# The experts of three routed layers, worked off with the four groups in turn instead of one group after the other

## The reference

```python
g_prob = softmax(t @ rg_w + rg_b); g_p, g_idx = top_k(g_prob, 1)      # one of 4 groups
e_logits = (t @ re_w + re_b).reshape(n_tok, 4, n_experts // 4)[own group]
e_p, e_idx = top_k(softmax(e_logits), 2)                              # two experts of that group
...
y = (silu(x @ w_gate[e]) * (x @ w_up[e])) @ w_down[e]                 # hidden width 512
out[token] += g_p * e_p / sum(e_p) * y
```

| layer | blocks of each expert | sum |
|---|---|---|
| 0 | 3 3 2 3 / 2 2 2 2 / 3 3 3 3 / 2 3 3 3 | 42 |
| 1 | 1 1 1 2 4 5 1 4 / 2 1 2 1 1 3 2 1 / 1 1 1 1 1 1 1 1 / 2 1 1 1 2 1 1 2 | 51 |
| 2 | 2 2 1 2 1 1 2 1 / 2 1 1 2 2 2 2 1 / 1 1 3 3 1 2 5 2 / 1 1 1 1 1 1 1 1 | 51 |

## Time and profile before

### The profile page before, as it was taken

The page is one execution under the profiler, slowest core; times in us unless marked ns, Lnnn a source line. Parts: engine busy times, 40 slices in busy tenths (PEclk is TensorE's granted clock), DMA queues, the critical chain, the costliest instruction groups (busy, mean ns, idle before and its releaser), DMA issues. The chain is left out here.

```text
span 2638.0 us, 87033 instructions
## 1 busy us (share of the span) xinstructions
PE 2273.6 (86%) x37784; PEld 1652.5 (63%) x37785; DVE 1061.3 (40%) x2686; ACT 549.8 (21%) x1197; POOL 290.6 (11%) x487
## 2 busy tenths in 40 slices
PE   8997988788899888999767779978889988788986
PEld 4445546566688655777545535868876466566763
DVE  1306442222553844333212257457675353222323
ACT  2126211111400731111001031034432111111111
POOL 1001223223100010000000010012333100000001
PEclk9998999999999999999989889989999999999998
DMA  8602169999404007979999942010001289999996
GB/s 339 268 32 96 50 242 337 410 382 366 171 32 155 9 19 296 382 292 428 429 429 428 427 151 72 33 58 3 3 5 66 88 343 428 428 428 428 409 428 249
DMA packets 92275, 635.63 MB, mean 241 GB/s; under 512 B 22741, under 2 KB 43481, under 8 KB 58090
## 3 DMA queue, kind: packets, MB, share of 16 engines
q1 hardware_dynamic: 48272, 584.61, 53.8%
q0 software_dynamic: 12752, 29.14, 3.5%
q10 hardware_dynamic: 31114, 19.86, 2.4%
HBM read 588.42 MB, written 45.12 MB: 240 GB/s over the span
## 5 line engine op out<-in xcount | busy, mean ns | idle before, releaser
L1323 PE MATMUL ps<-ring,arena 128*32 128x128 f32 x13184 | 410.7, 284 | 111.3 <-DMA ring<-in_experts 73.8
L1323 PEld LDWEIGHTS ps<-ring,arena 128*32 128x32 f32 x13184 | 380.8, 115 | 154.7 <-issue 74.2
L1534 DVE TENSOR_TENSOR arena<-arena,ps 128x64 f32<-128x64 f32 x292 | 64.8, 222 | 587.5 <-ACT arena L1382 587.5
L1382 ACT ACTIVATE arena<-ps 128x64 f32<-128x64 f32 x292 | 65.5, 224 | 1075.1 <-PE ps L1323 950.0
L1334 PE MATMUL ps<-ring,arena 128*32 128x256 f32 x3296 | 204.4, 382 | 35.1 <-DVE arena L1537 20.0
L1300 PE MATMUL ps<-x_tok,arena 128*32 128x256 f32 x3456 | 212.0, 384 | 14.7 <-DVE arena L1437 8.3
L1323 PE MATMUL ps<-arena 128*32 128x128 f32 x5504 | 174.4, 286 | 48.3 <-DMA arena<-in_experts 36.3
L1323 PEld LDWEIGHTS ps<-arena 128*32 128x32 f32 x5504 | 161.4, 115 | 67.5 <-DMA arena<-in_experts 42.3
L1334 PEld LDWEIGHTS ps<-ring,arena 128*32 128x32 f32 x3296 | 107.1, 110 | 111.3 <-issue 27.8
L1273 PE MATMUL ps<-ring,arena 128*128 128x512 f32 x384 | 172.0, 604 | 3.4 <-PEq L2861 1.7
L1300 PEld LDWEIGHTS ps<-x_tok,arena 128*32 128x32 f32 x3456 | 116.3, 112 | 72.4 <-issue 21.8
(11 more groups left out here) (506 smaller groups left out, 3234.9 us busy)
## 6 DMA issues: line engine op xcount, KB each, us to landing
ring<-in_experts SPq DMA_DIRECT2D x165, 2048.0 KB, 21.7
arena<-in_experts SPq DMA_DIRECT2D x50, 2048.0 KB, 24.3
xt_mem<-in_experts SPq DMA_DIRECT2D x25, 2048.0 KB
ring<-in_mixer_chunks SPq DMA_DIRECT2D x24, 2048.0 KB, 11.8
xybuf<-arena ACTq DMA_DIRECT2D x602, 32.0 KB, 6.8
xybuf<-arena SPq DMA_DIRECT2D x1, 9216.0 KB, 51.8
xbuf<-arena SPq DMA_DIRECT2D x1, 9216.0 KB, 31.7
arena<-xbuf POOLq DMA_DIRECT2D x168, 32.0 KB, 6.5
```

Of the source, the lines that this page charges most:

```text
L1323: ins = pe.matmul(ps[at, 2 + half, 0:P], xg[:, k, :], w_gu[half][:, k, q, :], start=(k == 0), stop=(k == NK - 1))
L1382: act.activation(silu_g[:, half, :], ps[:, 2 + half, 0:HALF], ACT.Silu).then_inc(s_silu[half], 1)
L1534: dve.tensor_tensor(hidden[:, half, :], silu_g[:, half, :], ps[:, 2 + half, HALF:P], ALU.mult)\
```

## The change

Two lines of data flow change. In `expert_chunks`, the experts of an array are put into the order: first expert of each of the four groups, second expert of each group, and so on (old number g·E/4+e moves to place 4e+g). In the router, the masked logits `es` are written in the same order, so that picks, counts, table, slots and loops follow it by themselves. The input `el` and the router's weights keep their order. No instruction, transfer, semaphore or loop is added or taken away; every expert keeps its tokens, its three chunks and its number of blocks, and the output is the same sum.

```diff
-                    link(dve.tensor_tensor(es.rearrange("p j (g e) -> p j g e", g=G),
+                    link(dve.tensor_tensor(es.rearrange("p j (e g) -> p j g e", g=G),
                                            el.rearrange("p j (g e) -> p j g e", g=G),
                                            pen.unsqueeze(3).to_broadcast([P, NT, G, EPG]), ALU.add))
...
-    return np.ascontiguousarray(np.concatenate([gu, dn], axis=1))
+    chunks = np.concatenate([gu, dn], axis=1)
+
+    return np.ascontiguousarray(chunks.reshape(4, E // 4, *chunks.shape[1:]).swapaxes(0, 1).reshape(chunks.shape))
```

## The result

The changed kernel takes 2620.43 us (median of 4 runs, 2612.69 to 2623.02) against 2642.53 us: ratio 0.9912, 95% interval 0.9894 to 0.9930. That is 22 us less, where 22.1 were forecast (2619.9 us). The profiled execution took 2620.4 us, its span is 2618.7.

The account below looks back on a forecast made before the run. The loops of layers 1 and 2 were taken as mostly bound by weight loads, losing time when the queue was empty. -23.3 + 1.2 + 0 + 0 = -22.1, so 2642.0 - 22.1 = 2619.9 us, range 2611 to 2629.

Parts of the forecast that it names:

- layer 1's term: Layer 1's expert loop: loads stop less at full buffers, empty queue falls to 5.4 us, -23.3 us.
- the heap: Heavy experts close together; layer 1's new one has 4, 1, 1, 2, 5, 3 blocks from place 16, 121 us against 91 of loads.
- The working: Expert-by-expert calculation of a loop from load and block prices and three buffers; layer 1 ends at 1516.2 old, 1492.9 new.
- the 15.15 us an expert: Price of loading one expert's weights in the loops: 14.7 + 0.3 per block, taken with the mean of 1.6 blocks.
- Layer 2: Layer 2's expert loop: the old order already fits, the new one costs +1.2 us, bounds -2 and +7.
- Layer 0: Layer 0's expert loop: load time is the same in any order, so 0 us, bounds -7 and +7.
- The rest: Strided `es` writes, mixer chunks and last stores behind layer 1, and gathers: 0 us, bounds -2 and +2 for the stores.
- The heap that moves with its holes: Rival: the queue may stand before layer 1's new heap too; half the gain goes, 2630 us or so; chance 0.08.
- The clock: Rival: five experts behind weight waits in layer 1 run first blocks in 10.8 instead of 7.0 us; 2638 us; chance 0.05.
- pay for even loads: Rival: layer 0's last 18 blocks take 7.6 instead of 6.2 us, 25 us more, time 2645 us; chance 0.04.
- nothing happens: Rival: layer 1's queue loss comes from elsewhere than full buffers, so the time stays 2642 us; chance 0.03.

Follow-up runs that it names:

- moving the heap: Groups in turn as in the changed kernel, but layer 1's experts reordered inside each group, heavy ones at places 4 to 12: 2637.35 us, ratio 0.9975.
- layer 2 alone: Groups in turn in layer 2 only, the other layers in the old order, against the kernel before: 2646.24 us, ratio 1.0011.
- the far orders: As the changed kernel, but layer 0's experts put heavy first (2619.13 us, median of three executions, a fourth took 8226) or light first (2625.06 us).
- 27.4 in the second: The unaltered changed kernel measured once more, on the chip of the two layer 0 order runs: 2615.03 us, ratio 0.9902 against 2642.46.
- layer 0 alone turned: Groups in turn in layer 0 only, the other layers in the old order, against the kernel before: 2640.53 us, ratio 0.9993.
- the fastest order: Changed kernel with the experts inside each group of layers 1 and 2 ordered for these inputs' counts by the working: 2603.54 us, ratio 0.9845.

## Why the prediction was right

*The mechanism, and layer 1's term.* Right, and now shown by moving the heap: the gain is queue time that full buffers had cost. Its size was somewhat too large: -23.3 expected, -19.2 in the first pair of profiles. Over all profiles the old order has 486.2, 487.6 and 489.0 us, the changed one 467.0, 466.8, 466.7, 466.8 and 466.5, so the difference of the means is 487.6 - 466.8 = 20.8 us. The working was too short for both orders, 483.7 and 460.4 us, and more so for the new one. The term that was mis-sized is first of all the 15.15 us an expert, taken as a constant. The prediction's own price was 14.7 + 0.3 per block, and in and behind the heap two blocks fall to an expert. From place 16 to place 27, 24 blocks of 12 experts, the working's 3.8 us of waiting taken off, I find 15.3 us each (1245.1 to 1432.7, both starts of waiting products). In the old order the heap's stores went out while the queue was empty anyway, and so cost nothing; this is argued, no run shows it by itself. With 14.7 plus 0.3 for each block copied in that time, the working gives 1516.2 and 1494.2, so -22.0. For the rest, 1 us against the means and 3 against the first pair, the profile shows three places. The queue is empty for 3.8 us in the first stretch, where the working had 1.6, and for 4.6 behind the heap, where it had 3.8. And the last expert, which starts 2.5 us behind the landing of its chunk (3.4 in the working), halts once more, for "issue", in its second half:

```profile
1481.86 1.95 PE L1323 MATMUL ps<-ring,arena 128*32 128x128 f32 x64 [0.17 <-issue]
...
1487.08 2.13 PE L1323 MATMUL ps<-ring,arena 128*32 128x128 f32 x33 [1.63 <-issue]
...
1493.10 3.76 PE L1323 MATMUL ps<-ring,arena 128*32 128x128 f32 x127
```

What it waits for there the profile does not name, and how much of the rest each of the three makes stays open.

*Layer 2.* Expected +1.2, bounds -2 and +7; measured +2.7 in the profiles, +2.9 in the medians with layer 2 alone. Right in sign. In the changed kernel the last 60.9 us run at 353 GB/s, and the loss has two parts:

```profile
2520.00:2530.00 10.00, 10.00 (x260) 7.60 (x254) 4.07 (x15) 1.96 (x4) 0.00 (x0) 1.00 0.79 291
...
2570.00:2580.90 10.90, 8.45 (x164) 5.29 (x156) 2.56 (x9) 0.45 (x2) 0.00 (x0) 0.84 0.36 144
```

Behind the heap of 3, 2, 5 the queue is empty for 10.0 × (1 - 291/428) = 3.2 us, as behind the old one (3.0). In the last 10.9 us, 7.2 go by with the loads over and TensorE still at its blocks. Before, the end lost 4.6:

```profile
2590.00:2600.00 10.00, 7.01 (x132) 4.64 (x128) 2.57 (x9) 0.45 (x2) 0.00 (x0) 0.76 0.56 230
```

The heap stands so late that TensorE hasn't worked it off when the last weights land.

*Layer 0.* Expected 0, bounds -7 and +7; measured -1.3 between the first profiles and 0.9993 (0.9983 to 1.0003) alone, so within the bounds. Over all profiles the loop has 288.1, 289.5, 289.6 us in the old order, 286.8, 287.8, 288.2, 289.6 and 280.8 with the groups in turn, and 285.1 and 287.8 in the far orders. The two far orders do not differ by more than one order does from execution to execution; the times above leave it open whether order costs some us here. That a block is dearer beside loads was read from the earlier trace rows; that this is why the order counts for so little is argued, not shown.

*The rest.* The wait for the last stores behind the loop of layer 1 was to stay as it was within 2 us; it went from 6.5 to 4.6. Writing `es` with a stride was taken as 0. It is dearer, as the same operation after shows against the earlier trace rows, but by some 0.1 us a layer:

```profile
L1469 DVE TENSOR_TENSOR arena<-small,arena x3: 273/387/396, 364.6 to 2101.4; 128x128 f32<-128x128 f32 x2, 128x64 f32<-128x64 f32 x1
```

*The sum.* 22.1 forecast, 22.1 in the first runs, 27.4 in the second (2642.46 - 2615.03). The two loops with a term in the sum come to -20.8 + 2.7 = -18.1 us over all profiles. In the first pair of profiles the 4 us missing in layer 1 were made up by a stretch between the loops that was 4.0 us shorter and for which the sum has no term. It came again in two of the three later profiles with layers 1 and 2 as changed, and its cause is open: to that extent the exact hit is luck.

*The rivals.* The heap that moves with its holes came true for 4.6 us, as worked out, and when it is put where it hurts it takes 16 of 21. The clock fell to 0.85 in the waits, and full blocks behind them took 6.95 us as before. The rival counted one head too many: by the prediction's own working place 20 does not begin behind a wait (start 1308, its chunk 1304). The Trainium skill ("TensorE: Matmul & The Clock Gate", section "HAM oscillation") is right that the clock falls there and that the products behind a wait pay (3.38 against 1.96 us for 64), but here the loads cover it. Layer 0 does not pay for even loads: its loop is 286.8 us, and 287.8 with layer 0 alone turned. That nothing happens is refuted.

## What to carry to other kernels

Where weights stream through a few buffers and the work per weight varies, the order of the items sets how long the queue stands empty. Two prices (the load of one item, the work of one unit) and the number of buffers were enough here to work out 486 and 467 us by hand to within 7. Rotating groups is a means only if it parts heavy items; in one layer it won 21 us, in the next it lost 3. A transfer that used to fall into a hole of the queue has its full price once the hole is closed. And the loop's end is the wrong mark to aim at where later work waits for its stores: the fastest order won 15.3 us in the loop of layer 1 and gave 8.9 back behind it.

## What was not expected of the hardware

A VectorE operation of 128 partitions x 128 float32 went from 292 ns to 387 and 396 when its output was written with a stride of four elements, and its smaller form (128 x 64) from 226 to 273.
